# Head 0's keys and first queries are loaded in the last rounds of the key/value phase

## The reference, cut to what matters

```python
kv_in = _rmsnorm(x, kv_norm)
k = (kv_in @ w_k).reshape(b, T, N_HEADS, HEAD_DIM)
v = (kv_in @ w_v).reshape(b, T, N_HEADS, HEAD_DIM)
proj = _rmsnorm(x, b_norm_pre[j]) @ b_w_in[j]
q, z = jnp.split(proj, 2, axis=-1)
...
z = jnp.einsum('bqhd,bkhd->bhqk', q, k) * scale
log_keep = jnp.where(causal, jax.nn.log_sigmoid(-z), 0.0)
rev = lax.cumsum(log_keep, axis=log_keep.ndim - 1, reverse=True)
...
a = jnp.exp(log_a)
o = jnp.einsum('bhqk,bkhd->bqhd', a, v)
...
h = (jax.nn.silu(z) * o.reshape(b, T, D_ATTN)) @ b_w_out[j]
x = x + _rmsnorm(h, b_norm_post[j])
```

## Time and profile before

| what | us |
|---|---|
| median of 3 runs (3093.34 to 3095.19) | 3094.89 |
| the profiled execution | 3094.63 |
| its span, first to last instruction | 3093.1 |
| PE busy | 2911.1 |
| DVE busy | 1603.2 |
| ACT busy | 1348.4 |
| POOL busy | 1208.0 |

### The profile page before, as it was taken

The page is one execution under the profiler, slowest core; times in us unless marked ns, Lnnn a source line. Parts: engine busy times, 40 slices in busy tenths (PEclk is TensorE's granted clock), DMA queues, the critical chain, the costliest instruction groups (busy, mean ns, idle before and its releaser), DMA issues. The chain is left out here.

```text
span 3093.1 us, 43662 instructions
## 1 busy us (share of the span) xinstructions
PE 2911.1 (94%) x15360; PEld 2533.9 (82%) x15360; DVE 1603.2 (52%) x2080; ACT 1348.4 (44%) x2783; POOL 1208.0 (39%) x1048
## 2 busy tenths in 40 slices
PE   6999999999799799999889999999999999988998
PEld 5999999999778699999677888888888878766776
DVE  5322122221234511010177888888888889885654
ACT  6000010010144411111266777777777788774332
POOL 2332232233000122222175757575757566651000
PEclk9999999999899899999889999999999999998999
DMA  4111111010344255453466767676666767847763
GB/s 141 41 28 35 35 35 42 20 35 28 124 129 137 74 173 169 132 168 127 126 204 189 231 179 227 184 218 193 207 204 190 215 205 216 259 137 221 233 212 110
DMA packets 295254, 450.98 MB, mean 146 GB/s; under 512 B 53538, under 2 KB 238114, under 8 KB 288324
## 3 DMA queue, kind: packets, MB, share of 16 engines
q1 hardware_dynamic: 282916, 405.11, 42.3%
q0 software_dynamic: 12192, 44.06, 4.8%
HBM read 325.29 MB, written 123.81 MB: 145 GB/s over the span
## 5 line engine op out<-in xcount | busy, mean ns | idle before, releaser
L1424 POOL TENSOR_TENSOR a_a<-a_a,a_prod 128x512 f32<-128x512 f32 (+4 forms) x640 | 667.4, 1052 | 418.1 <-DVE a_prod L1381 417.1
L1381 DVE TENSOR_TENSOR_SCAN a_prod<-a_keep,a_prod,a_unread 128x513 f32<-128x513 f32 x384 | 488.4, 1272 | 0.0
L318 PE MATMUL c_pg<-a_xh,c_wh 128*128 128x384 f32 (+1 forms) x1280 | 463.6, 362 | 5.9 <-POOL c_wl L253 5.9
L319 PE MATMUL c_pg<-a_xl,c_wh 128*128 128x384 f32 (+1 forms) x1280 | 462.1, 361 | 0.0
L320 PE MATMUL c_pg<-a_xh,c_wl 128*128 128x384 f32 (+1 forms) x1280 | 461.9, 361 | 0.0
L1388 DVE TENSOR_TENSOR a_atl<-a_pt,a_ath 128x512 fp32r<-128x512 f32 (+3 forms) x640 | 380.3, 598 | 153.2 <-ACT a_ath L1333 149.6
L1325 ACT ACTIVATE a_a<-a_pz 128x512 f32<-128x512 f32 (+3 forms) x640 | 351.8, 550 | 191.1 <-PE a_pz L1248 169.6
L1333 ACT ACTIVATE a_ath<-a_pt 128x512 fp32r<-128x512 f32 (+3 forms) x640 | 348.7, 556 | 108.6 <-PE a_pt L1273 107.6
L1273 PE MATMUL a_pt<-ident,a_a 128*128 128x128 f32 x2176 | 345.8, 274 | 16.2 <-POOL a_a L1424 9.4
L1326 ACT ACTIVATE a_keep<-a_pz 128x512 f32<-128x512 f32 (+3 forms) x640 | 352.9, 551 | 0.0
L1273 PEld LDWEIGHTS a_pt<-ident,a_a 128*128 128x128 f32 x2176 | 274.4, 141 | 68.7 <-POOL a_a L1424 19.9
(11 more groups left out here) (182 smaller groups left out, 5095.3 us busy)
## 6 DMA issues: line engine op xcount, KB each, us to landing
a_x<-x_d SPq DMA_DIRECT2D x96, 896.0 KB, 4.9
a_x<-x_d SPq DMA_DIRECT2D x64, 832.0 KB, 4.9
c_raw<-in_a_w_in POOLq DMA_DIRECT2D x32, 512.0 KB, 4.7
a_kh<-kh_t SPq DMA_DIRECT2D x30, 512.0 KB, 11.1
a_kl<-kl_t SPq DMA_DIRECT2D x30, 512.0 KB, 14.3
y_t<-c_sz SPq DMA_DIRECT2D x8, 1088.0 KB, 3.9
f_y_in<-y_t SPq DMA_DIRECT2D x17, 512.0 KB, 6.6
x<-f_xn POOLq DMA_DIRECT2D x17, 512.0 KB, 4.9
```

The costliest lines, as they stand in the source:

```text
L318: pe.matmul(out, w_h[:, kt, :], x_h[:, kt, r], start=(kt == 0), stop=False)
L319: pe.matmul(out, w_h[:, kt, :], x_l[:, kt, r], start=False, stop=False)
L1381: dve.tensor_tensor_scan(prod[:, s, 0:w][:, ::-1], keep[:, n % KS, 0:w][:, ::-1], unread[:, 0:1].broadcast_to([P, w]), start, ALU.mult, AL ...
L1424: pool.tensor_tensor(part, part, prod[:, n % PS, 1:w + 1], ALU.mult).then_inc(weighted, 1)
```

## The change

The streamed weights of all phases (raw, high, low and two gains) get one room that lives through the whole program (`w_room`); slot 0 serves q in the attention, slot 1's raw half serves z. q, kh and kl of head 0 move to the top of SBUF (`Early`), which stays free during the key/value phase. That allows four things:

- SP loads q (the last 512 tokens), kh and kl (all tokens) of head 0 after round 5 of the key/value phase (`load_first`), ahead of the stores of rounds 6 and 7. The rest of q is loaded in the attention.
- POOL splits the first q weights at the end of the key/value phase (one more `unit`), and fetches the first z weights there. The attention loads neither raw weights nor the gain at its start.
- The wait for the stores of the value rows moves from the end of the key/value phase into the attention, ahead of the load of v of head 0.
- In pair 0 the chunk places begin at column 300, not 4500. POOL splits z's weights only (from column 100), and v of head 0 after the first four pieces.

```diff
@@ phase_keys
+            for g in range(NG):
+                sp.wait_ge(hl_stored[g], 32 * 3)
+            apart(sp, passed_sp)
+            early.load_first(sp)
             for c in range(KT - 2, KT):
                 round_(c)
...
-            for s in range(2):
-                sp.wait_ge(rows_stored[s], 32 * NG * KT)
...
-            unit(KT, 0, gain_kv, None)
-            unit(KT, 1, gain_kv, None)
+            unit(KT, 0, gain_kv, lambda i: qz_v[:, :, Q, 2, :])
+            unit(KT, 1, gain_kv, lambda i: qz_v[:, :, Z, 0, :])
+            unit(KT + 1, 0, gain_b, None)
+            pool.wait_ge(raw_loaded[1], 16 * (KT + 1))
@@ chunks
-    first = 4500 if is_pair(pr, 0) else 2000 if gates(pr) == (Z,) else 0
+    first = 300 if is_pair(pr, 0) else 2000 if gates(pr) == (Z,) else 0
@@ schedule
-    own = [m for m in gates(pr) if m == Z or is_pair(pr, 0)]
-    items += [((1000 if is_pair(pr, 0) else 100) + 700 * (2 * k + half), 4, "weights", (m, half), 0)
-              for k, m in enumerate(own) for half in range(2)]
+    items += [(100 + 700 * half, 4, "weights", (Z, half), 0) for half in range(2)]
@@ class Early
+    def load_first(self, sp):
+        for dst, top, bottom in self.sources:
+            tokens = slice(FIRST_Q if dst is self.q else 0, SEQ)
+            for part, src in ((slice(0, HD), top), (slice(HD, P), bottom)):
+                sp.dma_start(dst[part, tokens].bitcast(F32), src[0:HD, tokens]).then_inc(self.first_loaded, 16)
@@ phase_attend, SP
-            load(0, 0, slice(SEQ - 2 * Z_W, SEQ), first_loaded)
-            load(0, 0, slice(0, SEQ - 2 * Z_W))
-            sp.dma_start(gain[:, :], gate_gain.rearrange("(kt p) -> p kt", p=P),
-                         allow_slow_non_contiguous=True).then_inc(gain_loaded, 16)
+            load_x(0, 0)
+            for s in range(2):
+                sp.wait_ge(early.rows_stored[s], 32 * NG * KT)
             load_v(0, 0)
-            load_raw(0)
-            for part in range(PARTS):
+            for part in range(1, PARTS):
                 load_x(0, part)
+            early.load_rest(sp, q_rest)
             load(0, 1)
             load_v(0, 1)
@@ phase_attend, POOL
+                if is_pair(pr, 0) and hh == 0 and n == QG:
+                    split_v(0, 0)
...
-            split_v(0, 0)
-            pool.wait_ge(gain_loaded, 16)
-            pool.wait_ge(ones_set, 1)
+            for done in (w_scaled[Q], w_hi[Q], w_ready[Q]):
+                pool.sem_inc(done, 2)
```

More of the change, by code:

```diff
@@ L1042, in phase_attend @@
         HK = KT // 2
-        q2 = [room(f"a_q{s}", [P, SEQ], F32R, ROOM[s] + 0) for s in range(2)]
-        kh2 = [room(f"a_kh{s}", [P, SEQ], F32R, ROOM[s] + 4 * SEQ) for s in range(2)]
-        kl2 = [room(f"a_kl{s}", [P, SEQ], F32R, ROOM[s] + 8 * SEQ) for s in range(2)]
-        v2 = [room("a_v0", [P, QT, 2, HD], F32R, ROOM[0] + 12 * SEQ), sb("a_v1", [P, QT, 2, HD], F32R)]
-        x = room("a_x", [P, PARTS, PART_KT, 2, PW], F32R, ROOM[2])
-        wh, wl = (sb("a_w" + n, [P, 2, KT, P], F32R) for n in "hl")
-        raw = sb("a_raw", [P, 2, KT, P])
-        gain = sb("a_gain", [P, KT])
+        at_late = lambda n, at: late(f"a_{n}1", [P, SEQ], F32R, at)
+        q2, kh2, kl2 = ([mine, at_late(n, i * 4 * SEQ)]
+                        for i, (n, mine) in enumerate((("q", early.q), ("kh", early.kh), ("kl", early.kl))))
+        v2 = [at_top("a_v0", [P, QT, 2, HD], F32R, V_AT), sb("a_v1", [P, QT, 2, HD], F32R)]
+        x = late("a_x", [P, PARTS, PART_KT, 2, PW], F32R, X_AT)
+        raw, (wh0,), (wl0,), (_, gain) = w_room
+        wh, wl = [wh0, sb("a_wh1", [P, KT, P], F32R)], [wl0, sb("a_wl1", [P, KT, P], F32R)]
         v_in = sb("a_v_in", [P, 2, QT, HD])
@@ L1057, in phase_attend @@
         o_sb = sb("a_o", [P, 2, QG * P])
-        qh_out, ql_out, gate = (room("a_" + n, [P, PW], dt, ROOM[2] + X_SIZE + i * PW * 4)
+        qh_out, ql_out, gate = (late("a_" + n, [P, PW], dt, X_AT + X_SIZE + i * PW * 4)
                                 for i, (n, dt) in enumerate((("qh_out", F32R), ("ql_out", F32R), ("gate", F32))))
@@ L1131, in _, with load @@
         def _(sp):
-            def load(pr, hh, tokens=slice(0, SEQ), done=None):
+            def load(pr, hh):
                 rows = bass.ds((2 * pr + hh) * HD, HD)
@@ L1169, in do @@
                     elif g == ORDER[-1] and hh == 0:
-                        ahead.load_weights(sp, range(KT - 2, KT))
+                        ahead.load_weights(sp, range(2))
                 elif what == "scored":
@@ L1179, in do @@
                     elif hh == 0:
-                        ahead.load_weights(sp, range(KT - 2))
+                        ahead.load_weights(sp, range(2, KT))
                     else:
@@ L1236, in score @@
                 i, p0, w = QG * g + q, kp * Z_W, piece_width(n)
-                first = is_pair(pr, 0) and hh == 0
-                if first and n == 0:
-                    pe.wait_ge(first_loaded, 96)
-                elif n == (2 * QG if first else 0):
-                    pe.wait_ge(qk_loaded[hh], 96 * (pr + 1))
+                if is_pair(pr, 0) and hh == 0:
+                    if n == 0:
+                        pe.wait_ge(early.first_loaded, 96)
+                    elif g == ORDER[1] and is_diagonal(u) and q == 0:
+                        pe.wait_ge(q_rest, 32)
+                elif n == 0:
+                    pe.wait_ge(qk_loaded[hh], 96 * (pr + hh))
                 pe.wait_ge(z_used, piece(pr, hh, n - ZS) + 1 + ZS)
@@ L1536, in phase_finish @@
         gain = sb("g_gain", [P, D])
-        yh = [sb(f"g_yh{s}", [P, KT, P], F32R) for s in range(2)]
-        yl = [sb(f"g_yl{s}", [P, KT, P], F32R) for s in range(2)]
+        yh, yl = ([at_weights(f"g_{n}{s}", [P, KT, P], F32R, (2 * i + s) * KT * P * 4) for s in range(2)]
+                  for i, n in enumerate(("yh", "yl")))
         xn = sb("g_xn", [P, D])
@@ new lines, in build @@
+            k_v, v_v, qz_v = kvq_views(w_k, w_v, b_w_in[0])
+            g_kv, g_b = (g[:, :] for g in w_room[3])
+            first = [(lambda c: qz_v[:, :, Q, 0, :], g_b), (lambda c: qz_v[:, :, Q, 1, :], g_b),
+                     (lambda c: k_v[:, :, c, :], g_kv)]
+            phase_out(nc, "f_", [y_t], a_w_out[0], a_norm_post[0], xp, xsm, ident, x1[0:SEQ, :], x1[SEQ:T, :],
+                      x32, begin_next=lambda pool, sem: begin_stream(
+                          pool, w_room, first, [kv_norm, b_norm_pre[0]], sem, "f_next_",
+                          sem("f_next_split")))
@@ L2031, in build @@
+            phase_keys(nc, k_v, v_v, qz_v, w_room, ident, x32, at_slab("b_xl", F32R), x_d, qh_t, ql_t, kh_t, kl_t,
+                       kp, vp, ks, vs, early)
         late_at = (nc.sbuf_base + 31) // 32 * 32
-        ctx.enter_context(nc.sbuf_tensor("late", [P, ROOM_SIZE // 4], F32))
+        ctx.enter_context(nc.sbuf_tensor("late", [P, LATE_SIZE // 4], F32))
         late = lambda name, shape, dt, at: nc.alloc_sbuf_tensor_at(name, shape, dt, offset=late_at + at)
         o_stored = sem2("a_o_stored")
-        ahead = Ahead(sem, sem2, late, qh_t, ql_t, kh_t, kl_t, cache_k.rearrange("b t h d -> b t (h d)"), oa_t, ob_t,
-                      sz_t, b_w_out[0], x1)
@@ L2037, in build @@
-        phase_attend(nc, x_d, qz_v, b_norm_pre[0], qh_t, ql_t, kh_t, kl_t, sz_t, vp, ident, identr, maskr, oa_t, ob_t,
-                     late, o_stored, ahead)
-        phase_finish(nc, ahead, cache_v.rearrange("b t h d -> b t (h d)"), vs, ident, identr, mask_sr, o_stored,
-                     b_norm_post[0], yp, ysm)
+        ahead = Ahead(sem, sem2, late, at_top, qh_t, ql_t, kh_t, kl_t, cache_k.rearrange("b t h d -> b t (h d)"), oa_t,
+                      ob_t, sz_t, b_w_out[0], x1)
+        phase_attend(nc, x_d, qz_v, w_room, qh_t, ql_t, kh_t, kl_t, sz_t, vp, ident, identr, maskr, oa_t, ob_t,
+                     late, at_top, early, o_stored, ahead)
```

93 lines of the change are left out of this document (54 added, 39 removed).

## The result

| | before | after |
|---|---|---|
| median of four runs each, us | 3094.11 | 3059.10 |
| lowest to highest, us | 3091.63 to 3095.19 | 3056.94 to 3061.77 |
| the profiled execution, us | 3094.63 | 3056.94 |
| its span, us | 3093.1 | 3055.4 |
| PE busy, us | 2911.1 | 2892.1 |

After to before is 0.9888, with a 95% interval of 0.9871 to 0.9905: 35.0 us faster. The sign was right, and the size was not.

What follows compares the result with a forecast made beforehand. PE's work was taken to set the time, so only its waits and half-clock stretches could be saved. Savings of 13.6 and 11.0 us, 24.6 in all, from 3094.63 gave a forecast of 3070 us, range 3065.5 to 3080.

Steps and rivals of the forecast that it cites:

- Part 1: Attention start: keys loaded early, first score at 1525.2 instead of 1535.25, 10.05 us sooner; the 4.40 us POOL wait goes.
- Part 2: First value block to score piece 16 of pair 0: piece 16 at 1554.5 against 1568.12, 13.6 us saved including the start.
- Part 3: Piece 16 of pair 0 to piece 16 of pair 1: 156.9 us instead of 167.90, 11.0 us saved.
- Part 4: Early loads, POOL's extra block, moved row wait and last phase's load order cost nothing (0 to 3 us, taken as 0).
- any loss ahead of 1522 us: Listed sign that the forecast is wrong: time lost before the attention, where the forecast expected no change.
- Late v: Rival at the attention's start: v lands 16.1 us after issue, 7.9 us lost, 3078 us; chance 0.10.
- The opening of the phase: Rival: barrier and code hold the first score at 1535.25, so 10.05 us are not saved, 3080; chance 0.03.
- The slower case: Key rounds 6 and 7: early loads hold row stores until PE stops; 3155 us at a 97 us hold; chance 0.03.

Runs made afterwards that it cites:

- a3: The kernel after with the six early loads of head 0 moved back to the head of the attention's SP queue: 3071.38 us.
- a4: The kernel after with v's split back at the head of POOL's queue, ahead of the first four score pieces: 3061.01 us.
- a5: The kernel after with pair 0's chunks spread from column 4500 again: 3073.66 us.
- p5: The kernel before with only pair 0's chunks spread from column 300 instead of 4500: 3089.94 us.
- p1: The kernel before with the streamed weights' room allocated ahead of the slab, as in after, and no instruction moved: 3087.18 us.
- p2: The kernel before with the weights' room placed as in after and the second weight slot also ahead of x: 3080.34 us.
- p3: The kernel before with 32 empty bytes ahead of the convolution's weight room: 3096.63 us.
- p4: The kernel before with 32 empty bytes ahead of the convolution's weight room and 32 more behind the gain: 3089.91 us.
- a2: The kernel after with the last phase's four tiles of split y back in the middle, as before: 3061.51 us.
- a9: After with both weight slots ahead of x, top tiles at a multiple of 64, and 2,752 empty bytes ahead of the last phase's high weights: 3054.24 us.

## Why the prediction was wrong, step by step

- **Part 1, the first score.** Right in mechanism, and a3 shows it: 3.27 us of idle ahead of the first score where the forecast leaves 2.83 (12.88 less 10.05). The nine scores took 10.04 us for 11.27, with the clock at half only up to about 1523, in their midst, where before it was at half through all nine.
- **Part 2, to piece 16.** The sum was right (32.6 us; the forecast was 1554.5 - 1521.83 = 32.7), its terms were not. I had 2.3 us of half clock, and there was none; I had 1.4 us of stall for POOL, and there were 1.76 and 2.00; the scores were 1.2 us quicker, and the start and the rest of the work as much longer. That these errors cancelled is luck. a4 shows that POOL paces this stretch, as the working had it.
- **Part 3, pair 0.** 154.5 for 156.9. I took the period of the next pair, which contains a stretch of 3.4 us at half clock at its end; pair 0 of after has none. That is most of the 2.4 us: a later pair of after takes 155.0 to 155.7 where it has none. My reason for the lost wait for x named two causes, wider chunk spacing and the order of transfers; a5 and p5 leave only the first.
- **Part 4 is the step that failed.** "What costs nothing" looked at instructions, queues and transfers, and there it was right: the stores were held up about as worked out (11.2 us to the landing, where 4.3 and 9.1 more make 13.4), ACT waited for them, and PE lost 0.0 us in after, up to 1.4 in the kernels next to it, of 0 to 3. (The landing of 4.3 us could not show by itself that a store waits for loads ahead of it; the 11.2 bear it out, though full transfer engines may have their part in them.) But part 4 did not look at where tiles lie. The kernel's room for streamed weights is allocated at another place, and after stands 8.6 us ahead at the last turn of the keys; placement alone (p1) is worth 7.3 us in the medians. I had written "any loss ahead of 1522 us" as a sign of being wrong, and that none of the terms of part 4 can be a gain: a gain had been excluded without a row that excluded it. As an estimate, the 3059.1 of after and these 7.3 make 3066.4, which the range holds; without placement the kernel would have stood near the range's lower end.
- **The later pairs, 4.3 us.** Not forecast. Windows of the clock at the ends of pairs, in before the first two of five and in after the first three:

```profile
1719.40:1722.80 3.40, 3.29 (x12) 3.00 (x13) 1.70 (x3) 1.42 (x3) 3.15 (x4) 0.50 1.01 219
1876.40:1879.80 3.40, 3.40 (x12) 3.07 (x13) 1.80 (x2) 1.68 (x3) 3.15 (x4) 0.50 1.01 217
```

```profile
1684.00:1687.40 3.40, 2.59 (x17) 2.41 (x18) 2.15 (x5) 1.69 (x3) 2.88 (x4) 1.00 1.04 231
1840.70:1844.10 3.40, 3.40 (x13) 2.98 (x12) 1.88 (x2) 1.69 (x3) 3.15 (x4) 0.50 1.00 213
1996.30:1999.70 3.40, 2.72 (x18) 2.54 (x19) 2.15 (x5) 1.69 (x3) 2.88 (x3) 1.00 1.04 230
```

  Ahead of these places PE idles for DVE and ACT, 1.0 us at most at a time, in both kernels alike. Before, p1, p2, p3 and p4 have a stretch at half clock at each pair's end (five or six in a row; p3 misses the first), and a pair takes 156.8 to 157.0 us; the kernels built on after have one at some ends only (after itself also at 2601.9 and 2728.2, where before has none), and a pair without it mostly takes 154.9 to 155.7. p5 misses the first and has the next three, but its later pairs take 1041.3 us together as in before. So this is not the places' doing alone, against what I expected of p5. What decides whether the clock falls at a pair's end stays open; it may also be what spreads the four runs of after over 5 us, which no trace here shows.
- **The last phase, 2.3 us lost.** The bigger part is its matmuls (816 of them, on average 2.4 ns further apart: 1.9 us), the rest the start of the phase, 16.14 us of idle for 15.79. Placement again (a2 and a9), and unforecast.
- **The rivals.** None of the four occurred. Late v began to cost at a landing of 10 us; v needed at most 8.8. The opening of the phase did not hold the first score. The slower case was far off, though its path is real: no wait of PE in rounds 6 and 7 of after, and 0.3 to 1.2 us in sum in seven of the eight other kernels with early loads.

a1 and a7, which are after with the second slot ahead of x, beat both kernels: 3053.7 and 3053.5 us.

## What to carry to other kernels

An edit that allocates tiles elsewhere can change the time of the matmuls that read them: print where each tile begins before and after, and count it as a term, of either sign. Measure it with the smallest edit, placement alone, before explaining a gain by the order of work. And what a place in the schedule gains is not additive: the same number in the place table was worth 4.8 us alone and 14.6 us with the parts that made room for it.

## What the runs showed of the hardware

- The distance between matmuls of equal shape at full clock depends on where the stationary and the moving tile begin relative to each other, in steps as small as 32 bytes: in the convolution 226 to 237 ns for 512 columns, 173 to 177 for 384. 64 empty bytes were worth 3.0 us in six rounds of it, and 4.2 us of 3094 in the medians (the interval has 1.5 to 7.7).
- It depends on the other tiles of the same row of matmuls too: with the low x alone of the tiles that they read moved, the 384-column spacing of the keys' high weights on the high x went from 181 to 174 ns, and moving only the low weights by 32 bytes changed that of the high weights on the low y in the last phase from 227 to 230 (a1, a7).
- The Trainium skill, "SBUF — State Buffer", in its section on who interferes with whom, gives TensorE two independent read ports, one for the moving operand and one for weights, and has it wait for nobody. By these runs the spacing of the same instructions still depends on the addresses of their tiles, 234 against 229 ns, and the measurement decides; whether the loss comes at these ports at all, no run here shows.
- In the keys the same differences do not give the same numbers throughout (slot 0 before: 64 modulo 128, and 233 ns), there with the low x 86,080 bytes below the high one. And in after slot 0 and both x lie at the very bytes of the convolution, and the three are 230, 229 and 230 ns for 229, 232 and 226: nearly the same sum, otherwise split. The table's rule holds for the convolution's tiles; a general one was not found.
- Stores issued behind 2.36 MB of loads in the same queue landed 11.2 us after their issue (after) where they took 4.7 without these loads (a3); the early loads cost the matmuls of that stretch 0.0 to 1.4 us of 102.2.
